# Scaling ahead of the weight split on VectorE, two more PSUM banks at a layer's start, and a softmax division moved ahead

## The reference

```python
# second block (one layer)
h = rmsnorm(x, g_mix) * (1 + scale1) + shift1
q, k, v, u, vs, ga, gb = split(h @ w_in)                # 4608 columns
y_attn = causal_attention(q, k, v) @ w_proj_attn        # 8 heads of 64, 256 tokens
y_sgu = spatial_gating(gelu(u), gelu(vs)) @ w_proj_sgu
x = x + gate1 * ((sigmoid(ga) * y_attn + sigmoid(gb) * y_sgu) @ w_out)
h = rmsnorm(x, g_ffn) * (1 + scale2) + shift2
x = x + gate2 * (square(relu(h @ w_ff1)) @ w_ff2)       # width 4096
x = rmsnorm(x, g_final)
# third block, for each of two layers
h = rmsnorm(x, pre_norm_g) * (1 + scale) + shift
q, k, v, g_att, u, b_gate, c_gate, g_conv = split(h @ w_in)   # 4096 columns
att = attention_with_bias(q, k, v) * silu(g_att)
cnv = b_gate * conv3(c_gate * u) * silu(g_conv)
x = x + gate * rmsnorm(concat(att, cnv) @ w_out, post_norm_g)
```

## Time and profile before

| | us |
|---|---|
| median of 3 runs | 2526.11 (2524.0 to 2530.88) |
| the profiled execution | 2521.12 |
| its span, first to last instruction | 2518.9 |
| TensorE busy | 1909.4 (76%) |
| VectorE busy | 733.8 (29%) |
| ScalarE busy | 540.6 (21%) |
| mean granted TensorE clock | 0.765 |

### The profile page before, as it was taken

The page is one execution under the profiler, slowest core; times in us unless marked ns, Lnnn a source line. Parts: engine busy times, 40 slices in busy tenths (PEclk is TensorE's granted clock), DMA queues, the critical chain, the costliest instruction groups (busy, mean ns, idle before and its releaser), DMA issues. The chain is left out here.

```text
span 2518.9 us, 34472 instructions
## 1 busy us (share of the span) xinstructions
PE 1909.4 (76%) x14694; PEld 1166.3 (46%) x14694; DVE 733.8 (29%) x1157; ACT 540.6 (21%) x860; POOL 54.5 (2%) x70
## 2 busy tenths in 40 slices
PE   6999886666666676766766677668897899887886
PEld 4886741222112111222111211237787889777876
DVE  4226620000000000000000000126445665547546
ACT  3420220000000000000000000015634554444543
POOL 0014000000000000000000000000000000000000
PEclk8999985666566656666566655678898999988988
DMA  8757489999999999999999999993334455434331
GB/s 339 272 193 295 168 326 423 425 426 425 426 425 425 426 426 425 425 426 425 426 425 426 425 426 425 425 383 103 123 105 130 143 176 181 146 104 131 104 109 40
DMA packets 153198, 760.53 MB, mean 302 GB/s; under 512 B 9719, under 2 KB 96503, under 8 KB 99480
## 3 DMA queue, kind: packets, MB, share of 16 engines
q1 hardware_dynamic: 149448, 754.07, 74.8%
q10 hardware_dynamic: 3664, 5.24, 0.6%
HBM read 756.13 MB, written 3.14 MB: 301 GB/s over the span
## 5 line engine op out<-in xcount | busy, mean ns | idle before, releaser
L900 PE MATMUL ps<-ring,arena 128*32 128x352 f32 x4096 | 622.5, 754 | 238.3 <-DMA ring<-in_w_exp_gate 131.3
L900 PEld LDWEIGHTS ps<-ring,arena 128*32 128x32 f32 x4096 | 147.1, 152 | 700.2 <-DMA ring<-in_w_exp_up 257.9
L913 PE MATMUL ps<-ring,arena 128*32 128x256 f32 x2816 | 235.5, 489 | 179.7 <-DMA ring<-in_w_exp_down 133.1
L1398 DVE TENSOR_TENSOR ring_lo<-ring,w_hi 128x1024 fp32r<-128x1024 f32 x220 | 268.2, 1224 | 314.4 <-ACT w_hi L1061 313.2
L624 PE MATMUL ps<-u_hi,w_hi 128*128 128x258 f32 x960 | 290.1, 302 | 25.7 <-DVE ring_lo L1398 25.7
L624 PE MATMUL ps<-u_hi,ring_lo 128*128 128x258 f32 x960 | 280.6, 292 | 0.0
L624 PE MATMUL ps<-u_lo,w_hi 128*128 128x258 f32 x960 | 279.5, 291 | 0.0
L913 PEld LDWEIGHTS ps<-ring,arena 128*32 128x32 f32 x2816 | 99.4, 135 | 323.9 <-DMA ring<-in_w_exp_down 185.5
L1061 ACT ACTIVATE w_hi<-ring 128x1024 fp32r<-128x1024 f32 x220 | 229.6, 1049 | 73.5 <-DMA ring<-in_w_in 36.9
L1732 DVE TENSOR_TENSOR arena<-arena,ps 128x704 f32<-128x704 f32 x15 | 13.3, 888 | 773.0 <-PE ps L900 773.0
L624 PEld LDWEIGHTS ps<-u_hi,w_hi 128*128 128x128 f32 x960 | 191.6, 200 | 42.4 <-DVE ring_lo L1398 32.3
(11 more groups left out here) (258 smaller groups left out, 1959.4 us busy)
## 6 DMA issues: line engine op xcount, KB each, us to landing
ring<-in_w_exp_gate SPq DMA_DIRECT2D x128, 1408.0 KB, 10.7
ring<-in_w_exp_up SPq DMA_DIRECT2D x128, 1408.0 KB, 10.9
ring<-in_w_exp_down SPq DMA_DIRECT2D x112, 1536.0 KB, 11.6
ring<-in_w_ada SPq DMA_DIRECT2D x48, 1536.0 KB, 8.7
ring<-in_w_in SPq DMA_DIRECT2D x38, 1536.0 KB, 7.1
ring<-in_w_ff SPq DMA_DIRECT2D x18, 1536.0 KB, 7.0
ring<-in_w_out SPq DMA_DIRECT2D x8, 1536.0 KB, 6.8
ring<-in_w_exp_down SPq DMA_DIRECT2D x16, 512.0 KB, 10.6
```

Of the source, the lines that this page charges most:

```text
L900: m = pe.matmul(ps[32 * j:32 * j + 32, 2 * (k // 8) + i, 0:FJ // 2], XCUR[:, k % 8, :], ring[:, s, at:at + FJ // 2], start=(k % 8 == 0), s ...
L913: m = pe.matmul(ps[32 * j:32 * j + 32, 4, 0:T], HIDT[:, c, :], ring[:, s, at:at + T], start=(c == 0), stop=(c == FC - 1), skip_group_check ...
L1398: tt(slot(c["u"], KD, c["w"], of=ring_lo)[:, :, at], slot(c["u"], KD, c["w"])[:, :, at], w_hi[:, s % HI, :, :].bitcast(F32), ALU.subtract) ...
```

## The change

On VectorE, block b is scaled before the low part of block b+3 is formed, in all three layers with a softmax and in `ff1`. `roots` and `row_roots` make the splits of blocks 3 and 4 (high parts up to 5) of the coming layer between the steps of the root. In `ff1` and `in3` the first two blocks are written to banks 6 and 7, and the fifth and sixth block then wait for no evacuation of them (`free`). The division of head h+1 is made one head earlier, and that of head 0 before the maximum of head 1. One block of each attention layer comes behind the last values (`TAIL`). The splits for `out2` are made between the units of `proj2`. `TMP` and `VF` get storage of their own, q and k of the third block other places, and the splits of attention tiles 0 to 2 for `out3` are made with the outputs of the pairs (`att_out`).

```diff
+TAIL = 1
...
+            for it in items:
+                it["bank"] = it["b"] % 4
+                it["free"] = it["b"] - 3
+            if n < WCOL // P:
+                for it, bank in zip(items, spare):
+                    it["bank"] = bank
...
+            if units and len(units) == 1:
+                for it in items[1:1 + len(spare)]:
+                    it["free"] -= 4
...
-    n = sum(len(g["items"]) for g in units) - QKV - FIRST_HEAD
+    n = sum(len(g["items"]) for g in units) - QKV - FIRST_HEAD - TAIL
     return [(FIRST_HEAD - 1, 1)] + [((n + ATT - 2 - h) // (ATT - 1) - 1, 1) for h in range(ATT - 1)]
...
+    ff1 = plan.dense(FF, lambda n: ["lat"], spare=(6, 7))
...
+        in3.append(plan.dense(FF, lambda n: ["lat"], flips=[(FLIP_AT, "v")], spare=(6, 7)))
...
+        TMP = sb("TMP", [P, 3, UCOL])
+        VF = sb("VF", [P, 4, T])
...
+        QA2 = ar(2 * K1, 4, T)
+        KA2 = ar(3 * K1, 4, T)
...
+        QA3 = ar(14 * K1, 4, T)
+        KA3 = ar(17 * K1, 4, T)
...
-                        pe.wait_ge(S("evacuated"), it["b"] - 3)
+                        pe.wait_ge(S("evacuated"), it["free"])
...
                         if it["b"] >= 4:
-                            pe.wait_ge(S("evacuated"), it["b"] - 3)
-                        bank = it["b"] % 4
+                            pe.wait_ge(S("evacuated"), it["free"])
+                        bank = it["bank"]
...
                     values(h)
+                for _ in range(TAIL):
+                    next(rest)
                 assert next(rest, 0) == 0
                 heads_done[0] += ATT
 
...
+            def roots(two, units=None):
+
+                if units is not None:
+                    high_parts(units[0]["items"][0]["s"] + HI + 1, group[0])
                 root_no[0] += 1
                 act.wait_ge(S("mean_square"), root_no[0])
                 mark(act.activation(rs[:, 0:T], rs[:, 0:T], ACT.Sqrt), "rooted")
+                if units is not None:
+                    high_parts(units[0]["items"][0]["s"] + HI + 2, group[0])
                 if two:
                     mark(act.activation(R_FIRST, R_FIRST, ACT.Sqrt), "rooted_first")
...
+                for _ in range(TAIL):
+                    next(rest)
...
+            for i, g in enumerate(proj2):
                 for it in g["items"]:
                     evacuate(it, (SQ, XN)[it["src"]][:, it["n"], :])
-            high_parts(starts["out2"] + 3)
+                high_parts(starts["out2"] + i + 1)
...
-            roots(False)
+            roots(False, ff1)
...
+                roots(l == 0, in3[l])
...
-            def row_roots(two):
+            def row_roots(two, units=None):
 
                 norms[0] += 1
+                if units is not None:
+                    low_parts(units[0]["items"][0]["s"] + HI)
                 waits("summed", norms[0])
                 if two:
                     link(ts(R_FIRST, ps[:, 5, 0:T], 1.0 / D, EPS, ALU.mult, ALU.add))
                     link(stt(rs[:, 0:T], R_FIRST, EPS, ps[:, 5, T:2 * T], ALU.mult, ALU.add), "mean_square")
                 else:
                     link(ts(rs[:, 0:T], ps[:, 5, 0:T], 1.0 / D, EPS, ALU.mult, ALU.add), "mean_square")
+                if units is not None:
+                    low_parts(units[0]["items"][0]["s"] + HI + 1)
                 waits("rooted", norms[0])
                 link(dve.reciprocal(rs[:, 0:T], rs[:, 0:T]))
...
             def scale_rows(it):
 
                 waits(*it["done"])
-                if it["b"] >= 3:
-                    waits("evacuated", it["b"] - 2)
-                mark(tt(TMP[:, it["b"] % 3, :], ps[:, it["b"] % 4, 0:UCOL], R, ALU.mult), "row_scaled")
+                waits("evacuated", it["b"] - 2)
+                mark(tt(TMP[:, it["b"] % 3, :], ps[:, it["bank"], 0:UCOL], R, ALU.mult), "row_scaled")
...
-            row_roots(True)
+            row_roots(True, in2)
...
                     for _ in range(k):
                         i, it = next(items)
                         if "flip" not in it:
+                            scale_rows(it)
                             low_parts(it["s"] + HI)
-                            scale_rows(it)
                         if gain is not None:
                             first_norm(i, gain)
...
                 low_ahead(QKV)
                 max_of(0)
+                divide(0)
                 for h in range(ATT):
                     if h + 1 < ATT:
                         max_of(h + 1)
-                    divide(h)
                     low_ahead(shares(units)[h][0])
+                    if h + 1 < ATT:
+                        divide(h + 1)
                     between(h)
                     low_ahead(shares(units)[h][1])
                     if h >= 2 and h % 2 == 0:
                         pair_out(h // 2 - 1)
                 pair_out(ATT // 2 - 1)
+                low_ahead(TAIL)
                 heads[0] += ATT
...
+            for i, g in enumerate(proj2):
+                if i > 0:
+                    low_parts(starts["out2"] + i, "ff1")
                 for it in g["items"]:
                     waits("evacuated", it["b"] + 1)
...
+            row_roots(False, ff1)
...
             for g in ff1:
                 for it in g["items"]:
+                    scale_rows(it)
                     low_parts(it["s"] + HI)
-                    scale_rows(it)
                     if previous is not None:
                         square_out(previous)
                     previous = it
...
+                row_roots(l == 0, in3[l])
...
+                def att_out(c):
+
+                    if c > 0:
+                        split(CAT3, c - 1)
+                    return tt(CAT3[:, c, :], ps[:, 7, 0:T], HQ[:, c, :], ALU.mult)
+
                 softmax(in3[l], lambda h: BIAS[:, h, :],
-                        lambda c: tt(CAT3[:, c, :], ps[:, 7, 0:T], HQ[:, c, :], ALU.mult), convolve,
+                        att_out, convolve,
                         "g_final_2" if l == 0 else None)
                 waits("evacuated", out_by(in3[l], 31))
-                split(CAT3, 0, 4)
+                split(CAT3, 3)
```

More of the change, by code:

```diff
@@ L148, in split, with dense @@
         return len(self.splits) - 1
-    def dense(self, cols, kinds, turned=(), after=lambda i: None, flips=()):
+    def dense(self, cols, kinds, turned=(), after=lambda i: None, flips=(), spare=()):
         units = []
@@ L225, in build @@
     out2 = plan.dense(D, lambda n: ["merged"])
-    ff1 = plan.dense(FF, lambda n: ["lat"])
+    ff1 = plan.dense(FF, lambda n: ["lat"], spare=(6, 7))
     ff2 = []
@@ L243, in build @@
     for _ in range(LAYERS3):
-        in3.append(plan.dense(FF, lambda n: ["lat"], flips=[(FLIP_AT, "v")]))
+        in3.append(plan.dense(FF, lambda n: ["lat"], flips=[(FLIP_AT, "v")], spare=(6, 7)))
         out3.append(plan.dense(D, lambda n: ["cat"]))
     starts = {"in1": in1[0]["items"][0]["s"], "out1": out1[0]["items"][0]["s"], "in2": in2[0]["items"][0]["s"],
-              "out2": out2[0]["items"][0]["s"], "end": len(plan.splits)}
+              "out2": out2[0]["items"][0]["s"], "ff1": ff1[0]["items"][0]["s"], "end": len(plan.splits)}
     ctx = ExitStack()
@@ L928, in _, with attention @@
             heads_done = [0]
-            def attention(rest, units):
+            def attention(rest, units, QA, KA):
                 for _ in range(QKV):
```

33 lines of the change are left out of this document (11 added, 22 removed).

## The result

| | before | after |
|---|---|---|
| median | 2525.06 us (2522.77 to 2530.88, 4 runs) | 2442.48 us (2437.54 to 2445.17, 4 runs) |
| ratio | | 0.9667, 95% interval 0.9643 to 0.9692 |
| the profiled execution | 2521.12 | 2445.17 |
| its span | 2518.9 | 2443.0 |
| TensorE busy / VectorE / ScalarE | 1909.4 / 733.8 / 540.6 | 1885.0 / 732.6 / 539.1 |

The change is worth 82.6 us by the medians where 65 were forecast; 2461 was predicted, and 2442.48 lies just outside the range, 0.5 us under its low end.

The account below looks back on a forecast made before the run. VectorE and ScalarE, waiting for each other by turns, were taken as the bound in ff1; 20+14+3+12+5.6+0.5+1.8-1.0+2+2.6+5 = 65.5 us off 2521.1 gives 2456, median 5 above: 2461. Range 2448 to 2474, or 2443 to 2488 with most of (a), near half of (b).

Parts of the forecast that it names:

- part 1: Softmax layers and ff1: scaling before the low part opens the VectorE-ScalarE loop; ff1 period 3.55 to 2.88 us, gain 20.
- Part 2, the starts: Layer starts: splits in the root and banks 6 and 7 shorten TensorE's waits; gain 14 us, plus 3 in in2.
- Part 3, attention: Attention: v's transposes gain 12 us, values 5.6 (in2) and 0.5 (block 3), out3 1.8, short waits 2; tail costs 1.0.
- one gain of 12: Three transposes of v in attention: 19.3 us of waits, 2.6 left each, 4 gained each; bounds 0 and 19.3.
- Part 4: Projection: splits for out2 under the projection's matmuls gain 2.6 us; own storage and other places for q and k, 0.
- The clock: TensorE's last third: about a third of the clock drops go; loss 30 us, gain taken 5, bounds 0 and 20.
- (a): Rival: only the steady chain and starts gain, attention's waits are moved, not shortened; gain 40 us, 2486; chance 0.22.
- (b): Rival: clock holds through most pauses (15 us more), v's transposes wait for nothing (7.3 more); 2438 us; chance 0.12.
- (c): Rival: VectorE's queue becomes the bound in ff1 and attention, period 4.45 us; +167 us, 2693; chance 0.02.
- (d): Rival: denser TensorE in ff1 is granted half the clock, 5.16 us a block; +47 us, 2528 in all; chance 0.02.
- (e): Rival: another wait ties VectorE and ScalarE, so the loop is not opened; no change, 2526 us; chance 0.02.
- the rule of the Trainium skill: Micro-idles between groups cycling through banks make the clock swing; by it, removing ff1's 0.39 us waits gives more than 20.

Follow-up runs that it names:

- output: Changed kernel with the output of a finished pair of heads moved right behind the next head's row maximum on VectorE: 2399.66 us, ratio 0.9504.

## Why the prediction was right and wrong

**What bounds it, and part 1: right in kind, and exact in ff1.** The two engines' loop was the bound, and opening it gives a period of 2.884 us and 20.1 us in ff1 and ff2 where 20 stood. In attention the prediction shared the effect of the order out over single waits. The order alone gives 73 us; of the sum's terms, 20, 12, 5.6, 0.5 and 2 rested on it, and the clock's 5 in part.

**Part 2, the starts: waits right, worth more.** Block 3 of ff1 and of each in3 starts at once; ff1 waits 1.14 us at block 5 (1.2 stood there). In2's block 4 waits 2.64 (2.6). The pieces were priced at 17 with the clock next to them; taking them out costs 24, and by the low clock more of it hangs on them (some 9 us, roughly) than the one block behind each pause.

**Part 3, attention: the waits right, one sign not seen.** Transposes of v 2.10, 2.10 and 1.31 (2.6 expected); values of in2 8.4 in all (7.6), of block 3 24.8 (25.5), the third ones 7.4 each (7.6); 1.11 before the spatial gating (1.0). The 2.6 came near by two errors that cancel. The items listed for it add up to 11.1 us; the 12.3 takes the first exponential twice, as 1.1 of its own and as VectorE's 1.2 of idle time. And VectorE's update of x, 0.4 a block for two blocks in in2 and the first in3, was left out:

```profile
1729.99 0.48 DVE L1578 SCALAR_TENSOR_TENSOR X<-X,vec,rs 128x256 f32<-128x256 f32 x1
```

Without the double count the wait is 1.4, with the update 2.2. The second in3 has no such update and waits 1.31, the others 2.10.

What the prediction booked as one gain of 12 is 19.3 us of waits gone by the order and 5.5 brought back by the division. That wait was booked as what is left over rather than as the price of an edit. The price, measured, is 11 us (6 to 17). Moving the splits of the attention tiles bought nothing that can be told. The wait at out3 went from 3.3 to 2.6 (2.4), and with those splits back at the end it is 2.9, so most of the change is not theirs.

**Part 4.** Out2's wait fell from 6.08 to 3.81 us (3.5). The storage, put at 0, gives 3 us in ff2 by the trace: the step failed by that much.

**The clock: the step that was mis-sized.** 5 us stood there, beside some 3 inside the price of the starts. In the profiled pair low clock went from 106 to 76 us, 13 us. That pair was an unlucky one to read: from in2 on, the kernel before and its three variants that differ only in storage or a pad have 106, 117, 114 and 113 us, and the changed kernel 76, 70 and 57. The means are 45 us apart, 20 us of time. So clock gave 13 in the pair and about 20 over these profiles, where 5 and 3 stood. The bounds of 0 and 20 held it; the value taken did not. The working had said that about a third of the drops should go, and that the loss is 30 us; a third of it is 10, and 5 was taken without a reason. That is the step that failed: in the pair 28% of the low clock went, over these profiles 40%. The medians agree, since they hold pauses and clock together: 24 us for 13 of waits (starts) and 43 for 30 (output), 45 to 85% on top; 11 for 8 (division) is too small to tell.

**The sum.** 65.5 were forecast for the profiled execution and 75.9 measured. Of the 10.4 missing, block 3 has 6.3 (27 with the clock's 5, and 33.3 measured; TensorE's idle time fell by 21.2 there and low clock from 63 to 38 us, 11 us, so some 2 of the 6.3 are waits and the rest is clock), ff1 and ff2 have 3.5 (the spacing in ff2), and 1.6 lie ahead of in2, where nothing changed; in2 and out2 gave 1.0 less than forecast. The other 8 of the 18.5 between 2461 and 2442.5 are the choice of execution: the profiled one of before lay 5 under its median, and I carried that 5 over, while the profiled one of after lies 2.7 above its own. The clock accounts for that: in in2, where the profiled pair has the same low clock before and after (28.5 and 28.9 us), the changed kernel with a pad has 12, and that alone is 7 us.

**The rivals.** (a), that the attention's waits are only moved, is refuted by the order alone: its in2 and in3 stretches fall by 16 to 19 us. (b) came nearest, 2438, with half its mechanism: the clock gave 5 more than forecast in the profiled pair and about 12 by the means above, where it wanted 15, and v's transposes wait for nothing only with the division back. That 2442.48 lies between the forecast and (b) is no credit to either sum. (c), (d) and (e) left no trace: VectorE has 0.5 us of slack a period and ff1's grant is 1.00. On the rule of the Trainium skill weighed there ("TensorE: Matmul & The Clock Gate", psum-queue depth-cycling): with the 26 waits of 0.33 to 0.40 gone, the grant in ff1 went from 0.99 to 1.00 and its low clock from 3 us to 0, worth 1.3 us. The trace disagrees with that rule for this layer.

**Parts, as measured.** Order 73 as the only edit and 68 as the last one, starts 24, division -11; the splits of the attention tiles -3 and the storage 3 are within what can be told. With the order at 73 or 68 the three make 86 or 81 for 83 measured; `TAIL` (1.1 us of wait before the gating) and the splits for out2 (2.3 us) were not taken apart, and how the parts share the clock wasn't either.

## What to carry to other kernels

Where two engines each wait more than 200 us for the other in one list of waits, read one period of both queues side by side: swapping two instructions that don't need each other was worth 68 to 73 of 83 us here, and no instruction got shorter. Price an edit of a queue's order by everything behind it on both engines: the division moved ahead delayed the next exponential, and with it ScalarE's next split. And when a pause of TensorE goes, count the half-clock stretch behind it, 45 to 85% on top in the two cases that are large enough to tell here, and look which waits are left: the nine of the values were worth 43 us more, for one call moved up.

## What the runs showed of the hardware

A pause's length alone doesn't say whether the clock drops. In the kernel with the order alone the values of two heads of the same layer wait 2.08 us each. TensorE's timeline at both, and the 8 us behind each (columns as in the earlier trace rows):

```profile
2179.84 1.79 PE L967 MATMUL ps<-arena 128*64 128x256 f32 x4 [2.08 <-DVE arena L1916]
...
2207.78 1.05 PE L967 MATMUL ps<-arena 128*64 128x256 f32 x4 [2.08 <-DVE arena L1916]
```

```profile
2180.00:2188.00 8.00, 8.00 (x33) 6.06 (x33) 2.42 (x6) 2.04 (x5) 0.00 (x0) 0.57 0.01 2
2208.00:2216.00 8.00, 8.00 (x59) 7.13 (x58) 4.07 (x8) 3.87 (x8) 0.00 (x0) 1.00 0.16 51
```

The same pause is followed by 33 matmuls at 1.2 GHz for most of the stretch the first time, and by 59 at 2.4 GHz the second. What tells the two apart these runs do not show.

The distance of matmuls at full clock is not a constant of their shape: 0.1167 or 0.1128 us in ff2 for the same instructions, by where the arrays lie, while pads of 24, 256 and 7168 bytes changed nothing.

Three profiles of the changed kernel (one with a pad) have the same idle time of TensorE from in2 on, 76.7 to 77.1 us, and spans of 2434.7, 2439.9 and 2443.0; 57, 70 and 76 us of low clock account for it. A term under some 8 us is read from the waits or from medians, not from one pair of spans, and low clock of a single profile says little about an edit.
